# Smaller steps in a two-block layer on one core: norms by quarters, a forget gate in pieces, split modulation weights

## The reference, cut to what matters

```python
# block 1
h = rmsnorm(x) ; q, k, v, u = split(h @ w_in)
attn = sliding_window_attention(q, k, v)          # 16 heads, 2 query tiles
ssm  = s5(u)                                      # 64 groups, sin/cos turns and a scan
x = x + concat(rmsnorm(attn), rmsnorm(ssm)) @ w_out
x = x + square(relu(rmsnorm(x) @ w_up)) @ w_down
# block 2
mod = silu(c) @ w_ada + b_ada                     # 6 x 2048 values for c, and for c_ctx
proj = modulate(x) @ w_in2                        # 256 tokens and 256 context tokens
hg = gated linear attention with a forget gate    # 8 heads, forward and backward
dn = gated delta rule                             # 8 heads, forward and backward
hy = long convolution
x = layernorm(ALPHA * x + g1 * (merge(hy, hg, dn) @ w_out2))
x = layernorm(ALPHA * x + g2 * (square(relu(modulate(x) @ w_ff1)) @ w_ff2))
```

## Time and profile before

| | us |
|---|---|
| median of 3 runs | 4836.05 (4824.05 to 4843.54) |
| the profiled execution: its own time | 4831.38 |
| the profiled execution: its span | 4829.9 |

### The profile page before, as it was taken

One profiled execution on the slowest core, in us unless ns is written; L12 is line 12 of the kernel. 1 busy time (PEld: TensorE's weight loads), 2 busy tenths in 40 slices (PEclk: granted clock), 3 DMA queues, 4 the chain that ended last, 5 costly groups with the idle time before them and its releaser, 6 DMA issues.

```text
span 4829.9 us, 69715 instructions
## 1 busy us (share of the span) xinstructions
PE 4297.8 (89%) x28096; PEld 3672.5 (76%) x28096; DVE 2806.8 (58%) x5619; ACT 1541.7 (32%) x2681; POOL 0.2 (0%) x4
## 2 busy tenths in 40 slices
PE   7989996999999899999877778777788997999997
PEld 7433334999999888898767777777555897999997
DVE  4666664565565432244667777777523566655654
ACT  3211112444444332243222223222100343444442
POOL 0000000000000000000000000000000000000000
PEclk9999998999999999998989999988898998999998
DMA  5744453565665544464631112111422653555553
GB/s 174 246 138 137 143 171 124 157 188 188 187 186 188 178 118 122 122 182 138 185 88 54 53 55 62 56 53 35 133 67 66 199 192 116 182 193 184 182 193 108
DMA packets 383056, 669.52 MB, mean 139 GB/s; under 512 B 43897, under 2 KB 77402, under 8 KB 382220
## 3 DMA queue, kind: packets, MB, share of 16 engines
q1 hardware_dynamic: 327168, 595.74, 41.0%
q10 hardware_dynamic: 55564, 69.31, 4.4%
HBM read 634.87 MB, written 29.46 MB: 138 GB/s over the span
## 4 chain that ended last, share of the span: by engine, by line
PE 65%; DVE 13%; issue 2%; ACT 2%; DMA 1%; ACTq 0%; DVEq 0%
PE acc L546 13%; PE acc L548 13%; PE acc L547 13%; PE acc L588 9%; PE bank L547 2%; PE bank L546 2%; PE bank L548 2%; PE bank L1683 2%; PE bank L1692 2%; PE bank L1690 1%; ACT weights_hi L510 1%; PE bank L2159 1%; DVE arena L1522 1%; PE acc L1491 1%; PE bank L733 1%
## 5 line engine op out<-in xcount | busy, mean ns | idle before, releaser
L525 DVE TENSOR_TENSOR weights_lo<-weights_ring,weights_hi 128x512 fp32r<-128x512 f32 x1600 | 1093.5, 691 | 1021.7 <-ACT weights_hi L510 1020.3
L510 ACT ACTIVATE weights_hi<-weights_ring 128x512 fp32r<-128x512 f32 x1600 | 992.9, 629 | 1079.9 <-PE acc L548 882.0
L547 PE MATMUL acc<-arena_halves,weights_hi 128*128 128x256 f32 (+2 forms) x3136 | 916.3, 292 | 0.0
L546 PE MATMUL acc<-arena_halves,weights_lo 128*128 128x256 f32 (+1 forms) x2944 | 861.4, 293 | 21.3 <-DVE weights_lo L525 11.7
L548 PE MATMUL acc<-arena_halves,weights_hi 128*128 128x256 f32 (+1 forms) x2944 | 859.1, 292 | 0.0
L546 PE MATMUL acc<-moving_halves,weights_lo 128*128 128x256 f32 (+1 forms) x2816 | 791.6, 281 | 72.7 <-DVE weights_lo L525 72.0
L548 PE MATMUL acc<-moving_halves,weights_hi 128*128 128x256 f32 (+1 forms) x2816 | 785.9, 279 | 0.0
L547 PE MATMUL acc<-moving_halves,weights_hi 128*128 128x256 f32 x2624 | 730.6, 278 | 0.0
L547 PEld LDWEIGHTS acc<-arena_halves,weights_hi 128*128 128x128 f32 x3136 | 590.6, 188 | 12.2
L546 PEld LDWEIGHTS acc<-moving_halves,weights_lo 128*128 128x128 f32 x2816 | 534.5, 190 | 81.3 <-DVE weights_lo L525 53.3
L588 PE MATMUL acc<-moving,weights_ring 128*128 128x256 f32 x2304 | 579.4, 397 | 10.6 <-ACT arena L691 9.4
(11 more groups left out here) (423 smaller groups left out, 4827.7 us busy)
## 6 DMA issues: line engine op xcount, KB each, us to landing
weights_ring<-in_w_in SPq DMA_DIRECT2D x624, 256.0 KB, 2.7
weights_ring<-in_w_ff SPq DMA_DIRECT2D x512, 256.0 KB, 3.0
weights_ring<-in_w_ada SPq DMA_DIRECT2D x384, 256.0 KB, 3.0
weights_ring<-in_w_up SPq DMA_DIRECT2D x256, 256.0 KB, 2.9
weights_ring<-in_w_down SPq DMA_DIRECT2D x256, 256.0 KB, 3.3
weights_ring<-in_w_out SPq DMA_DIRECT2D x128, 256.0 KB, 3.2
weights_ring<-in_w_branch SPq DMA_DIRECT2D x96, 256.0 KB, 3.4
s_state<-arena ACTq DMA_DIRECT2D x36, 256.0 KB, 2.8
```

Of the source, the lines that this page charges most:

```text
L510: a.activation(whi, k.slot(g.ring0 + kc), ACT.Copy).then_inc(*s.made("scalar_done", "high", n))
L525: v.tensor_tensor(wlo, k.slot(g.ring0 + kc), whi.bitcast(F32), ALU.subtract).then_inc(*s.made("vector_done", "low", n))
L546: pe.matmul(g.out[m], wlo[:, cols], xhi, start=first, stop=False, skip_group_check=g.shared)
L547: pe.matmul(g.out[m], whi[:, cols], xlo, start=False, stop=False, skip_group_check=g.shared)
```

## The change

**Norms by quarters.** Squares are made four chunks at a time, and TensorE sums a quarter as soon as it is there; the subtraction of the mean goes by quarters too, and the bias of a layernorm is added by ScalarE, chunk by chunk, beside VectorE's scaling. The tokens are loaded in quarters ahead of the constants, of which only the first 384 columns are awaited; the output is stored in quarters by SP.

**Modulation.** Groups 6, 8, ... 22 take the split form with 4 stationary columns (high and low half of `cc`), two products for each chunk instead of one whole product. Their halves are made in background steps: ScalarE's high in step s, VectorE's low in step s + 1, TensorE's products in step s + 2; such a group has 19 steps instead of 17. All groups now give 4 rows, which are transposed and added at the end.

**Attention.** The three copies out of PSUM for each tile are made by ScalarE instead of VectorE.

**Head stage.** The reciprocal goes tile by tile with a phase for each, and the elementwise work is spread over four more phases. dn starts at once and hg 8 phases later; each head of both chains is filled up to 58 phases; the quota is 475. The core of the diff:

```diff
+SPLIT_MODS = (6, 8, 10, 12, 14, 16, 18, 20, 22)
...
-            add("w_ada", n, io["w_ada"], n, KD, 0, None)
+            add("w_ada", n, io["w_ada"], n, KD, 0, None, **(dict(high=lambda kc: self.cc_halves[:, kc, :]) if n in SPLIT_MODS else {}))
...
+    for q in range(chunks // 4):
+        if ready:
+            a.wait_ge(*s.at(ready, tag, q))
+        a.activation(squares[:, 4 * q:4 * q + 4, :], src[:, 4 * q:4 * q + 4, :], ACT.Square).then_inc(
+            *s.made("scalar_done", "squares", tag, q))
...
+        if c % 4 == 0:
+            pe.wait_ge(*s.at("squares", tag, c // 4))
...
-    a.dma_start(k.params[:, :], io["params"]).then_inc(*s.landed("inputs"))
-    a.dma_start(k.consts[:, :], io["consts"]).then_inc(*s.landed("inputs"))
-    a.dma_start(k.res[:, :, :], io["hT"].rearrange("(c p) t -> p c t", p=P)).then_inc(*s.landed("inputs", "inputs"))
-    a.wait_ge(*s.at("inputs"))
+    tokens = io["hT"].rearrange("(c p) t -> p c t", p=P)
+    for q in range(4):
+        a.dma_start(k.res[:, 4 * q:4 * q + 4, :], tokens[:, 4 * q:4 * q + 4, :]).then_inc(*s.landed("tokens%d" % q, "tokens_in", "rms1", q))
+    a.dma_start(k.consts[:, 0:FIRST_CONSTS], io["consts"][:, 0:FIRST_CONSTS]).then_inc(*s.landed("first_consts", "first_consts"))
+    a.dma_start(k.params[:, :], io["params"]).then_inc(*s.landed("params", "params"))
+    a.dma_start(k.consts[:, FIRST_CONSTS:], io["consts"][:, FIRST_CONSTS:]).then_inc(*s.landed("consts", "consts"))
+    squares_scalar(k, "rms1", k.res[:, :, :], k.squares1, KD, L, "tokens_in")
+    a.wait_ge(*s.at("params"))
     a.activation(k.cc_sig[:, :], k.p("c"), ACT.Sigmoid).then_inc(*s.made("scalar_done", "cc_sig"))
-    squares_scalar(k, "rms1", k.res[:, :, :], k.squares1, L)
     split_scalar(k, k.some("w_in", *range(5)), {0: operand_scalar("w_in", lambda kc: k.squares1[:, kc, :])})
...
+    v.wait_ge(*s.at("cc_sig"))
+    serial(k, v.memset(k.cc_whole[:, :, :], 0.0))
+    pair = lambda x: x.rearrange("p (c m) -> p c m", m=2)
+    v.tensor_tensor(k.cc_whole[:, :, 0:2], pair(k.p("c")), pair(k.cc_sig[:, :]), ALU.mult).then_inc(*s.made("vector_done", "cc"))
+    v.wait_ge(*s.at("cc_high"))
+    v.tensor_tensor(k.cc_halves[:, :, 2:4], k.cc_whole[:, :, 0:2], k.cc_halves[:, :, 0:2].bitcast(F32), ALU.subtract).then_inc(
+        *s.made("vector_done", "cc_low"))
...
-        v.wait_ge(*s.at("probs_t", n))
-        own(v.tensor_copy(pt[:, 0:2 * P], ps_s[:, 0:2 * P]))
-        own(v.tensor_copy(pt[0:16, 2 * P:], ps_s[0:16, 2 * P:3 * P]), "probs_copied", n)
-        yield
-        v.wait_ge(*s.at("values", n))
-        own(copy(k, k.attn[half:half + 64, 2 * kv + hh // 2, P * qt:P * qt + P], ps_o[half:half + 64, 0:P]), "attended", n)
...
+        a.wait_ge(*s.at("probs_t", n))
+        a.activation(pt[:, 0:2 * P], ps_s[:, 0:2 * P], ACT.Copy).then_inc(*s.made("scalar_done"))
+        a.activation(pt[0:16, 2 * P:], ps_s[0:16, 2 * P:3 * P], ACT.Copy).then_inc(*s.made("scalar_done", "probs_copied", n))
+        yield
+        a.wait_ge(*s.at("values", n))
+        a.activation(k.attn[half:half + 64, 2 * kv + hh // 2, P * qt:P * qt + P], ps_o[half:half + 64, 0:P], ACT.Copy).then_inc(
+            *s.made("scalar_done", "attended", n))
...
+    if g.split:
+        yield
+        yield
     for name, index in g.before:
         pe.wait_ge(*s.at("drained", name, index))
     for kc in range(g.kchunks):
-        pe.wait_ge(*s.at("weights", g.ring0 + kc))
-        mm = pe.matmul(g.out[0], ccv[:, kc, :], k.slot(g.ring0 + kc), start=kc == 0, stop=kc == g.kchunks - 1)
-        mm.then_inc(*s.made("tensor_done", "ring_free", g.ring0 + kc))
+        first, last = kc == 0, kc == g.kchunks - 1
+        if g.split:
+            n, whi, wlo = halves(k, g, kc)
+            pe.wait_ge(*s.at("low", n))
+            pe.matmul(g.out[0], g.high(kc), wlo, start=first, stop=False)
+            pe.matmul(g.out[0], g.high(kc), whi, start=False, stop=last).then_inc(*s.made("tensor_done", "halves_used", n))
+        else:
+            pe.wait_ge(*s.at("weights", g.ring0 + kc))
+            pe.matmul(g.out[0], k.cc_whole[:, kc, :], k.slot(g.ring0 + kc), start=first, stop=last).then_inc(
+                *s.made("tensor_done", "ring_free", g.ring0 + kc))
...
 def modulation_scalar(k, g):
     a, s = k.nc.scalar, k.s
-    for _ in range(17):
-        yield
+    if g.split:
+        for kc in range(g.kchunks):
+            n, whi, wlo = halves(k, g, kc)
+            a.wait_ge(*s.at("weights", g.ring0 + kc))
+            a.wait_ge(*s.at("halves_used", n - k.HALVES))
+            a.activation(whi, k.slot(g.ring0 + kc), ACT.Copy).then_inc(*s.made("scalar_done", "high", n))
+            yield
+        yield
+        yield
+    else:
+        for _ in range(g.kchunks):
+            yield
+    yield
...
 def modulation_vector(k, g):
-    for _ in range(17):
-        yield
+    v, s = k.nc.vector, k.s
+    if g.split:
+        yield
+        for kc in range(g.kchunks):
+            n, whi, wlo = halves(k, g, kc)
+            v.wait_ge(*s.at("high", n))
+            v.tensor_tensor(wlo, k.slot(g.ring0 + kc), whi.bitcast(F32), ALU.subtract).then_inc(*s.made("vector_done", "low", n))
+            s.mark("vector_done", "ring_free", g.ring0 + kc)
+            yield
+        yield
+    else:
+        for _ in range(g.kchunks):
+            yield
+    yield
...
-    groups = [(modulation(k, k.groups["w_ada", n]), 17) for n in range(24)]
+    groups = [(modulation(k, k.groups["w_ada", n]), 19 if n in SPLIT_MODS else 17) for n in range(24)]
...
-    for r in range(2):
+    rows = k.mix[0:96, 0:4, 0:P]
+    for r in range(4):
...
-    for _ in range(7):
+    for _ in range(13):
...
-    own(v.reciprocal(f, f))
+    for j in range(NT):
+        if j:
+            yield
+        own(v.reciprocal(f[:, j, :], f[:, j, :]))
     v.wait_ge(*own.last)
     own(v.tensor_tensor(kk, e1, f, ALU.mult))
+    yield
...
+        if j == 2:
+            yield
         own(v.tensor_tensor_scan(cm[:, j, 1:P + 1], k.ones_row, f[:, j, :], 0.0, ALU.mult, ALU.add))
...
-        yield from lockstep(before + [strand(k, r, head) for r in range(2)] + [start(k, head)])
+        phases = 0
+        for _ in lockstep(before + [strand(k, r, head) for r in range(2)] + [start(k, head)]):
+            phases += 1
+            yield
+        for _ in range(58 - phases):
+            yield
     yield from end(k, name, 7)
 def heads2(k, hg_start, forget, dn_start, delta, end, whole):
-    chains = [chain(k, "hg", hg_start, forget, end), chain(k, "dn", dn_start, delta, end, 18)]
-    beside(lockstep(chains), 414, [(whole(k, g), 36) for g in k.some("read", 11, 12) + k.some("gates", *range(6))])
+    chains = [chain(k, "hg", hg_start, forget, end, 8), chain(k, "dn", dn_start, delta, end)]
+    beside(lockstep(chains), 475, [(whole(k, g), 36) for g in k.some("read", 11, 12) + k.some("gates", *range(6))])
...
+def layernorm_scalar(k, tag, x, squares, bias):
+    a, s = k.nc.scalar, k.s
+    squares_scalar(k, tag, x, squares, KD, T, "centred")
+    for c in range(KD):
+        a.wait_ge(*s.at("scaled", tag, c))
+        a.activation(x[:, c, :], x[:, c, :], ACT.Identity, bias=bias[:, c:c + 1]).then_inc(*s.made("scalar_done", "normed", tag, c))
+
...
-    v.tensor_tensor(x, x, rs.unsqueeze(1).broadcast_to((P, KD, T)), ALU.subtract).then_inc(*s.made("vector_done", "centred", tag))
+    for q in range(4):
+        part = x[:, 4 * q:4 * q + 4, :]
+        v.tensor_tensor(part, part, rs.unsqueeze(1).broadcast_to((P, 4, T)), ALU.subtract).then_inc(
+            *s.made("vector_done", "centred", tag, q))
...
-        v.scalar_tensor_tensor(x[:, c, :], x[:, c, :], gain[:, c:c + 1], rs, ALU.mult, ALU.mult).then_inc(*s.made("vector_done"))
-    v.wait_ge(*s.now("vector_done"))
-    for c in range(KD):
-        v.tensor_scalar(x[:, c, :], x[:, c, :], bias[:, c:c + 1], None, ALU.add, ALU.bypass).then_inc(*s.made("vector_done"))
+        v.scalar_tensor_tensor(x[:, c, :], x[:, c, :], gain[:, c:c + 1], rs, ALU.mult, ALU.mult).then_inc(
+            *s.made("vector_done", "scaled", tag, c))
...
+    for q in range(4):
+        part = slice(4 * q, 4 * q + 4)
+        sp.wait_ge(*s.at("normed", "ln2", 4 * q + 3))
+        sp.dma_start(k.io["out"].rearrange("(c p) t -> p c t", p=P)[:, part, :], k.res[:, part, NMETA:]).then_inc(*s.landed("out"))
```

73 lines of the change are left out of this document (38 added, 35 removed).

## The result

The changed kernel takes 4850.0 us (median of 15 runs, 4838.7 to 4864.8), the kernel before 4831.8 in the same series. The ratio is 1.004, 95% interval 1.0028 to 1.0051. The interval is about 6 us wide on either side, so that the change is clear of noise; the forecast had reckoned with 24. The profiled execution's span is 4863.4 us against 4829.9, so 33.5 us longer; it is the slowest of the fifteen (4864.8 us), so some 15 of these 33.5 us aren't in the median.

The account below looks back on a forecast made before the run. No engine alone: TensorE nearly full in attention beside VectorE with 198 us spare, order of work in the head stage. 4831.4 + 57 - 60 - 34 = 4794 us, median 4799; range 4700 to 4890.

Parts of the forecast that it names:

- the attention stage's term: Attention stage with nine split modulation groups: +57 us in sum, between -70 (-58 - 12) and +110.
- the ring: Split groups' exchange pieces: VectorE's turn, low half, TensorE's products and "driven" wait in a circle; 29 pieces pay 1.5 us, +43.
- the clock as a rival of its own: Attention stage: TensorE's clock falls to 1.2 GHz half of the time in closed-ring pieces; +24, 4823 us; chance 0.12.
- The lows in the other pieces: Attention stage, the other 29 pieces: VectorE's low halves take 47 us, of which waits can hide 28; +19 us.
- The relief of TensorE: Attention stage: split products save TensorE 58 us of 284; used as lower bound if nothing but TensorE counts.
- The copies: Attention stage: moving copies to ScalarE takes 31 us off VectorE; between 0 and -31, taken as -12 us.
- Whole groups' pieces: Attention stage, sixty pieces of unsplit groups: 0.13 more chunk each at 0.86 us; +7 us.
- Head stage: Eight heads: forget gate's front laid on dn's levels, hg eight phases behind; 7.5 us a head, -60; bounds -158 and +45.
- Small stages: Layernorms -20.6, norms -2.7 and -1.8, start -8, store -3.7, added rows and instructions +3; sum -34 us.
- The halves didn't hide: Rival, attention stage: halves hide in waits elsewhere in a channel; stage -30 instead of +57, 4712 us; chance 0.22.
- Phases didn't cost latency: Rival, head stage: 475 phases bring more engine waits; slower overall from 1.96 us a phase, 4902 us at 2.10; chance 0.15.
- The split form's products are as short as reckoned: Rival, modulation: four-column fp32r products cost 0.43 us like plain f32, not 0.23 apart; +12, 4811 us; chance 0.03.

Follow-up runs that it names:

- the fillers: Changed kernel with two products of zeros by 128 constants added ahead of each split product's wait: 4858.9 us, ratio 1.0053; with four: 4868.1 us, 1.0076.
- half of the columns: Kernel without split groups, whole product covering 256 of 512 columns in the nine groups, so part of the modulation is left out: 4715.9 us, ratio 0.9768.
- The new order: Changed kernel with VectorE and ScalarE taking a piece's modulation steps ahead of the exchange's step, TensorE's order kept: 4788.2 us, ratio 0.9898.

## Why the prediction was wrong

The step that failed is the attention stage's term, +57 us in the forecast's sum and +136 measured. Its miss of 79 us is larger than the whole forecast gain of 37, and turned the sign of the change. The other terms came to -102.5 us where -94 was forecast.

**Attention stage: +57 forecast, +136 measured.** The sign of the term and its mechanism, the ring, were right; these sizes were not.

- *The ring, +43 forecast.* 29 pieces by 1.5 us; measured 30 pieces by 2.20: +66. In the piece shown the links on VectorE were right to 0.05 us; those on TensorE were taken at 2.4 GHz from the earlier trace rows, and at a granted clock of 0.50 they took 1.18 us more. At the 0.69 that the thirty pieces had on average, TensorE was at the lower level for 0.62 of the time: 1.18 x 0.62 x 30 = 22 us, an estimate, and 23 to 40 by the fillers. Two more sizes were off in it and cancel in part: the closed pieces take 5.15 us even at 0.95 (with the fillers), where I had 4.7, and the same pieces before take 3.88 us on average, where I had 3.2, from pieces at 664 us, when attention's own products had ended (the last L888 starts at 633 us). My prediction had the clock as a rival of its own (+24, 0.12), and that size was right. It shouldn't have been a rival: the forecast's own mechanism brings it about. A ring in which TensorE is busy for 1.7 of 4.7 us is of the same kind as the stretch of the earlier trace rows with a third busy and a clock of 0.66, and the row was there to be used in the sum. The Trainium skill, "TensorE: Matmul & The Clock Gate", § What's actually happening, has the low level as the default that activity releases. The runs agree: the stage has 0.96 unsplit, 0.91 with half of the columns and 0.79 with the closed ring, and 0.91 again with fillers.
- *The lows in the other pieces, +19 forecast.* Measured +70 for all pieces of split groups without an exchange. I took VectorE's idle time of the channel's output as cover (28 us; 4.3 of eight channels give 26) and charged the rest. VectorE's subtractions alone cost 44 us of the stage, 7 of them in exchange pieces (4.11 us instead of 3.88, 29 pieces); so the term is 33 to 37 where I had 19. The high halves, costed at nothing since ScalarE was busy 89 of 530 us, take 14. The remaining 20 or so I put down to TensorE in the chain there too: I had the ring close only in exchange pieces, but attention's steps hand over between the same three engines. That last share is a difference of measured numbers, and its cause is not shown by a run of its own. The new order took only some 8 of the 70 away.
- *The relief of TensorE.* It was in no term of the sum, only in the lower bound, as -58; it is worth -20 where the halves cost nothing. That bound stood too low: TensorE, busy 92% of the stage, wasn't alone its bound.
- *The copies, -12 forecast:* 0 (+3 to -6). *Whole groups' pieces, +7 forecast:* 0.3.

**Head stage: -60 forecast, -52.5 in the changed kernel's trace, -66 without split groups.** Right; the two differ by no more than the scatter, and the median of twelve kernels gives -57. With -52.5, 902.5 us over 475 phases is 1.90 a phase, forecast 1.88, below the 1.96 from which the rival decided. The reason also holds, the front laid on the other chain's levels: TensorE is busy for 23.55 of 30 us there, where it was for 10.34. What the forecast didn't see is that the chains drifted against one another before, by 25 us over the stage.

**Small stages: -34 forecast.** Measured -9.3, -9.3, -10.7 and -14.2, -43.5 in all. The layernorms and the store are right to half a microsecond in this trace, and to 3 us in those of the other kernels. The start gave as much as forecast although its sum waits for constants and not for tokens. Whether the norms of the second -9.3 gave their 4.5 can't be told within a scatter of 20 us, nor do the 6.5 us between the layernorms need a cause.

**The rivals.** The halves didn't hide: split groups never came out ahead, open ring or closed. The Trainium skill, "Perfetto Trace Analysis", § Optimization Strategy, counts the interleaving of regimes with different most-contended engines as a possible gain. My prediction claimed that for the halves, but they move work within one regime, and that was a loss of 58 us even with the ring open; the head stage is the case that the page speaks of, a front on VectorE laid beside levels on TensorE, and there the offset gained 73 us (4791.6 to 4718.1). Phases didn't cost latency. The split form's products are as short as reckoned: with four stationary columns they start 0.23 us apart in the kernel with the ring opened, too (410.72 and 410.95 us), where a plain f32 instruction takes 0.43.

## What to carry to other kernels

Before moving work from a full engine to one with idle time, ask where in that engine's queue it will stand, and who waits for what is behind it: 99 us of subtractions on an engine that idled 198 of 530 us cost 44. A background strand should not be the same-piece input of a foreground engine; here the order within a piece alone was worth 78 us. And price an engine's links in a new ring at the clock that the ring will leave it, not at the clock of the dense stage in which they were measured. For interleaved chains, try the offset before the granularity: here it was worth 73 us, and the granularity some 10. Before reading a few microseconds out of a pair of traces, see how much stretches of the same code differ between them.

## What was unexpected of the hardware

Added work made a stage shorter: 270 products of zeros took the granted clock from 0.79 to 0.91 and 23 us off the stage, while TensorE's busy time rose from 501 to 528 us; the whole program didn't get shorter by it. TensorE's busy time is no measure of its work: with 58 of 284 us of modulation work taken away, as reckoned, the stage showed 501 us busy against 489. And the clock can stay low without a long pause: from 271 to 311 us of the changed kernel, in a split group, it was 0.67 on average, and the longest pauses of TensorE there were six of 1.8 to 2.6 us.
